# An eleventh ring slot for expert rows, paid for by halved gate matrices, shared mixer rows and four sets of V weights

## What is computed

```python
h = h + mixer(rmsnorm(h))          # RG-LRU group and mLSTM group side by side, one W_in, one W_out
h = h + peer(rmsnorm(h))           # 8 heads, 16 experts of 16384 each
y = rmsnorm(h)

# peer, for a block of 128 tokens
qh = (xb @ wq).reshape(128, 8, 2, 128)
s1, s2 = qh[:, :, 0] @ keys1.T, qh[:, :, 1] @ keys2.T     # top 16 of each, then top 16 of the 256 sums
act = gelu(einsum('td,thkd->thk', xb, u_tab[e])) * softmax(sc)
out = einsum('thk,thkd->td', act, v_tab[e])

# in the mixer's RG-LRU group: gates of 8 blocks of 64 channels
r = sigmoid(einsum('btni,nij->btnj', xb, wa) + ba);  i = sigmoid(einsum('btni,nij->btnj', xb, wx) + bx)
```

## Time and profile before

| | us |
|---|---|
| median of 3 runs | 3149.01 |
| lowest and highest run | 3145.65, 3157.63 |
| the profiled execution | 3160.47 |
| its span from first to last instruction | 3158.7 |
| PE busy | 2558.1 (81%) |
| DVE busy | 2189.3 (69%) |
| POOL busy | 2020.1 (64%) |
| ACT busy | 689.3 (22%) |

### The profile page before, as it was taken

The page is one execution under the profiler, slowest core; times in us unless marked ns, Lnnn a source line. Parts: engine busy times, 40 slices in busy tenths (PEclk is TensorE's granted clock), DMA queues, the critical chain, the costliest instruction groups (busy, mean ns, idle before and its releaser), DMA issues.

```text
span 3158.7 us, 39239 instructions
## 1 busy us (share of the span) xinstructions
PE 2558.1 (81%) x11988; PEld 1176.9 (37%) x11988; DVE 2189.3 (69%) x5635; ACT 689.3 (22%) x2526; POOL 2020.1 (64%) x2131
## 2 busy tenths in 40 slices
PE   7787889777888789777888888777987788877666
PEld 2554444233523354233523353234523353333111
DVE  2364887588756877588757887588757877688453
ACT  2121222112311122112311222112221222111112
POOL 0131667766777667766777667766776667766775
PEclk9789999988988889988988899888988899877667
DMA  7363999999999999999999999999999999999998
GB/s 268 132 204 133 384 396 400 419 419 398 391 407 419 412 382 404 419 419 395 399 418 419 418 398 400 419 418 387 401 419 419 411 394 419 418 418 380 417 420 363
DMA packets 339982, 1212.73 MB, mean 384 GB/s; under 512 B 41064, under 2 KB 41200, under 8 KB 339776
## 3 DMA queue, kind: packets, MB, share of 16 engines
q0 software_dynamic: 304128, 1107.43, 87.7%
q1 hardware_dynamic: 35648, 102.80, 8.4%
HBM read 1205.21 MB, written 4.87 MB: 383 GB/s over the span
## 4 chain that ended last, share of the span: by engine, by line
PE 37%; DMA 28%; DVE 14%; issue 10%; POOL 7%; ACT 3%; POOLq 0%; SPq 0%; DVEq 0%; ACTq 0%
PE bank L487 22%; DMA ring<-peer_v,idxv 21%; PE acc L487 14%; DMA ring<-peer_u,idx 7%; POOL ring L463 7%; DVE ring L1510 5%; ACT xn L904 1%; DVE xc L1368 1%; ACT coefv L904 1%; DVE topi L1287 1%; DVE kw L1285 1%; DVE tops L1286 0%; DVE tops L1284 0%; DVE topi L1288 0%; ACT wv L904 0%
## 5 line engine op out<-in xcount | busy, mean ns | idle before, releaser
L487 PE MATMUL acc<-ring,wv 128*32 128x512 f32 x4224 | 1276.2, 708 | 488.4 <-DMA ring<-peer_v,idxv 370.0
L1510 DVE SCALAR_TENSOR_TENSOR ring<-ring,xcur 128x1024 f32<-128x1024 f32 x1056 | 1282.7, 1219 | 543.8 <-DMA ring<-peer_u,idx 527.6
L463 POOL DMA_INDIRECT ring<-peer_u,idx x1056 | 1015.6, 962 | 626.0 <-issue 403.1
L463 POOL DMA_INDIRECT ring<-peer_v,idxv x1024 | 970.4, 948 | 444.0 <-issue 264.3
L487 PEld LDWEIGHTS acc<-ring,wv 128*32 128x32 f32 x4224 | 170.1, 115 | 1135.9 <-DMA ring<-peer_v,idxv 840.6
L487 PEld LDWEIGHTS bank<-xT,win 128*128 128x128 f32 (+1 forms) x2304 | 277.1, 191 | 100.4 <-issue 95.5
L487 PE MATMUL bank<-xT,win 128*128 128x128 f32 (+1 forms) x2304 | 308.0, 291 | 3.9 <-ACT xT L904 2.4
L904 ACT ACTIVATE wv<-rep,coefv 128x32 f32<-128x32 f32 x1024 | 258.8, 312 | 53.2 <-PE acc L487 51.6
L487 PEld LDWEIGHTS bank<-xT,qk 128*128 128x128 f32 x1024 | 159.5, 246 | 86.3 <-issue 86.3
L487 PE MATMUL bank<-win,xT 128*128 128x512 f32 (+3 forms) x368 | 187.8, 645 | 1.9 <-ACT xT L904 1.9
L487 PE MATMUL bank<-xT,qk 128*128 128x128 f32 x1024 | 172.3, 337 | 0.1
(11 more groups left out here) (231 smaller groups left out, 2251.2 us busy)
## 6 DMA issues: line engine op xcount, KB each, us to landing
qk<-wq SPq DMA_DIRECT2D x64, 512.0 KB, 6.5
t<-wq SPq DMA_DIRECT2D x64, 512.0 KB, 6.8
ring<-peer_u,idx POOLq DMA_INDIRECT x1056, 7.6
ring<-peer_v,idxv POOLq DMA_INDIRECT x1024, 7.7
win<-w_in SPq DMA_DIRECT2D x6, 2048.0 KB, 15.1
ring<-wq SPq DMA_DIRECT2D x16, 512.0 KB, 5.0
wout<-w_out SPq DMA_DIRECT2D x1, 4096.0 KB, 21.5
xn<-x_prompt SPq DMA_DIRECT2D x8, 512.0 KB
```

The costliest lines, as they stand in the source:

```text
L463: pool.indirect_dma_start(out=ring[:, slot, :], out_offset=None, in_=(peer_u, peer_v)[which], in_offset=bass.IndirectOffsetOnAxis(ap=rows_ ...
L487: return nc.tensor.matmul(out, lhsT, rhs, start=start, stop=stop)
L1510: stt(row, row, 1.0, xcur[:, :], ALU.mult, ALU.mult, accum_out=dots[:, column(b, e):column(b, e) + 1]).then_inc(s_dot, 1)
```

## The change

The ring gets an eleventh slot. The 4 KB per partition for it come from four places. `wa` and `wx` are held without their zeros, as 64 columns for each half of the partitions, so that each 128-channel product becomes two products of 64 rows and 64 columns, which write the upper and the lower half of the same bank. The two rows of `rows_hi` move into `xl`, the convolution's input, behind its first three columns. `wv` has four sets instead of eight. `ones4` is one column that is read with a step of zero. The two memsets of `wa` and `wx` and SP's wait for them go.

```diff
-RING = 10
-SETS = 8
+RING = 11
+SETS = 4
...
-        wa = sb("wa", [P, FT, P])
-        wx = sb("wx", [P, FT, P])
+        wa = sb("wa", [P, FT, P // 2])
+        wx = sb("wx", [P, FT, P // 2])
...
-        ones4 = sb("ones4", [HEADS, P])
+        ones4 = sb("ones4", [HEADS, 1])
...
-        rows_hi = sb("rows_hi", [HEADS, 2, P])
...
-        rows = [kflat[0:HEADS, P * r:P * r + P] for r in range(4)] + [rows_hi[:, 0, :], rows_hi[:, 1, :]]
+        rows = [kflat[0:HEADS, P * r:P * r + P] for r in range(4)] + [xl[0:HEADS, f, CONV_W - 1:CONV_W - 1 + P] for f in range(2)]
...
-            sp.wait_ge(s_zero, 2)
             for half in range(2):
                 lo = half * 64
-                sp.dma_start(wa[lo:lo + 64, :, lo:lo + 64], lru_wa[half]).then_inc(s_blocks, 16)
-                sp.dma_start(wx[lo:lo + 64, :, lo:lo + 64], lru_wx[half]).then_inc(s_blocks, 16)
+                sp.dma_start(wa[lo:lo + 64, :, :], lru_wa[half]).then_inc(s_blocks, 16)
+                sp.dma_start(wx[lo:lo + 64, :, :], lru_wx[half]).then_inc(s_blocks, 16)
...
-            pool.memset(wa[:, :, :], 0.0).then_inc(s_zero, 1)
-            pool.memset(wx[:, :, :], 0.0).then_inc(s_zero, 1)
...
-                    for f in range(FT):
-                        mm(by4(bA)[:, f, 0:n], wa[:, f, :], xc[:, f, 0:n])
-                    for f in range(FT):
-                        last = mm(by4(bB)[:, f, 0:n], wx[:, f, :], xc[:, f, 0:n])
+                    for to, w_gate in ((bA, wa), (bB, wx)):
+                        for f in range(FT):
+                            for lo in (0, 64):
+                                own = slice(lo, lo + 64)
+                                last = mm(by4(to)[own, f, 0:n], w_gate[own, f, :], xc[own, f, 0:n])
                     last.then_inc(s_ri_ps, 1)
...
-                    mm(bD[:, 16:20], ones4[:, :], dg4[:, :]).then_inc(s_cols_ps, 1)
+                    mm(bD[:, 16:20], spread(ones4[:, :], 1, P), dg4[:, :]).then_inc(s_cols_ps, 1)
```

More of the change, by code:

```diff
@@ L198, in program @@
         s_state_out = sem("s_state_out")
-        s_zero = sem("s_zero")
         s_blocks = sem("s_blocks")
@@ L1382, in mixer @@
                     link(stt(rows[1][:, 0:n], rows[0][:, 0:n], 0.0, rows[1][:, 0:n], ALU.max, ALU.add))
-                    link(dve.tensor_tensor_scan(rows[2][:, 0:n], ones4[:, 0:n], rows[1][:, 0:n], 0.0, ALU.mult, ALU.subtract))
+                    link(dve.tensor_tensor_scan(rows[2][:, 0:n], spread(ones4[:, :], 1, n), rows[1][:, 0:n], 0.0, ALU.mult, ALU.subtract))
                     link(stt(rows[3][:, 0:n], bB[0:HEADS, 0:n], bg[:, 0:1], rows[2][:, 0:n], ALU.add, ALU.subtract))
```

## The result

The changed kernel takes 3193.49 us (median of 4 runs, 3191.95 to 3194.92) against 3150.0 us of the kernel before (4 runs). The ratio, taken over the runs, is 1.0125, 95% interval [1.0105, 1.0144], so it is slower by 1.05 to 1.44%; the medians lie 43 us apart. 3134 us was forecast, and the range, 3116 to 3151, doesn't hold the result.

What follows compares the result with a forecast made beforehand. Transfers at 419 GB/s were taken as the bound, POOL's gather issue second. Terms -9.9 - 5.0 - 2.5 + 2.2 = -15.2 us, taken from the median 3149.01, gave 3134 us; range 3116 to 3151.

Steps and rivals of the forecast that it cites:

- I take 419 as what the transfers can do here: Loop transfers: ceiling 419 GB/s against a rate of 408, so 65 us is all that better gather supply could win.
- Small rows in the convolution's buffer, one-column ones, no memsets: Moved rows, one-column ones and two dropped memsets: same instructions, no wait added, 0 us.
- the only slower one: Rival: gate halves don't overlap their weight loads, 14.9 us a step instead of 2.2; 3157 to 3246 us, chance 0.08.
- Eleven slots: Ring: POOL stands one gather further on when held, 1.24 us once a run; -17.4 us, bounds 0 and -23.
- A: Low-rate stretch at ticks 37 to 50, in each of 8 blocks, losing 3.9 to 7.9 us; gain 9.9 us.
- C: Low-rate stretch at tick 82, in 4 blocks, losing 1.6 to 2.1 us; gain 5.0 us, bounds 0 and 8.1.
- D: Low-rate stretch at ticks 20 to 26, in 4 blocks, losing 0.9 to 1.5 us; gain 2.5 us.
- rival 1: No gain from the slot: POOL's gain before tick 50 is waited away afterwards; 3146 to 3151 us, chance 0.25.
- Gate halves: Gate step on PE, 8 matmuls become 16: +1.1 us a step, +2.2 us for two startup steps.
- sets: ACT's V-weight copies wait for the set four experts back, not eight; covered by ACT's own wait, 0 us.
- POOL's wait for PE falls: Sign that the forecast is right: POOL's loop wait for PE, 179.7 us before, gets smaller.
- about 410: Sign that the forecast is right: the loop's mean rate rises from 408 to about 410 GB/s.

Runs made afterwards that it cites:

- e1: Changed kernel with the 32-byte constant eps allocated last, so the eleven-slot ring starts on a 256-byte boundary: 3145.7 us, 0.9973 of the kernel before.
- e5: e1 with the ring back at ten slots, leaving gate halves, four sets and small rows: 3152.93 us, 0.9998 of the kernel before.
- e6: Kernel before with 256 bytes of small constants moved behind the ring, which then starts at 575 x 256: 3154.96 us, 0.9989 of before.
- e8: Kernel before with a 32-byte pad behind the ring, so only what follows the ring starts off the boundary: 3153.42 us, 0.9991 of before.
- e9: e1 with five sets of V weights instead of four, gl_a and gl_b moved to the end of memory: 3141.48 us, 0.9964 of the kernel before.
- e10: e1 with the 128-byte rep allocated first, so win and wout start on a boundary too: 3145.26 us, 0.9972 of the kernel before.
- e3: Kernel before with a 128-byte pad ahead of its ten-slot ring: 3203.46 us, 1.0159 of the kernel before.

## Why the prediction was wrong

**The step that failed** is its first: "I take 419 as what the transfers can do here". It is read rightly for the kernel before. It was then carried into the changed kernel as a constant, with bytes and rate untouched, and the whole sum was about the 65 us that lie below it. But 419 is the rate for rows that start on a 256-byte boundary; off it the rate is 409. The 60 us that the lower ceiling costs in the loop, 34 to 41 net, are in no term of the sum. They came in by the edits that were costed at 0 or only for their instructions: "Small rows in the convolution's buffer, one-column ones, no memsets" and the gate halves. 2048 of the 2528 bytes are a multiple of 256, so that the one-column ones alone, 480 bytes less, made the offset. For an edit that changes a buffer's size, the instructions are not all: every buffer behind it moves. No rival held this either; the only slower one was on the weight loads.

**Eleven slots**, -17.4 us (bounds 0 and -23): right in sign, the size about half, 8 us with an uncertainty of 7, and, as will be seen, not in the places that it was added up from. In e1, where the ceiling is as before, A, C and D can be read one by one. Stretches of e1, columns as in the earlier trace rows:

```profile
725.00:734.00 9.00, 6.00 (x38) 2.32 (x36) 7.18 (x27) 1.55 (x6) 6.86 (x8) 1.00 1.02 366
...
1238.00:1251.00 13.00, 11.60 (x66) 5.31 (x64) 9.08 (x21) 3.90 (x13) 9.03 (x10) 1.00 0.95 342
1594.00:1607.00 13.00, 10.73 (x64) 5.30 (x64) 9.23 (x22) 3.90 (x13) 9.17 (x10) 0.99 0.91 323
1841.00:1874.00 33.00, 28.25 (x198) 20.09 (x196) 28.43 (x76) 6.93 (x28) 23.09 (x25) 0.90 0.99 372
...
2185.00:2229.00 44.00, 37.79 (x241) 25.05 (x241) 37.22 (x106) 9.73 (x39) 29.21 (x31) 0.86 0.96 354
```

- A, 1.24 us in each of 8 blocks: block 4 loses 33 x (1 - 372/419) = 3.7 us, before 3.9; block 5 44 x (1 - 354/419) = 6.8, before 7.9. The sign is right and the gain is 0.2 and 1.1 in these two blocks.
- C, -5.0: not there. Block 2 loses 13 x (1 - 342/419) = 2.4 us, before 1.6 to 2.1 where there was a dip; block 3, which had none (417), loses 13 x (1 - 323/419) = 3.0.
- D, -2.5: block 1 loses 9 x (1 - 366/419) = 1.1 us, before 1.5; a gain of 0.4 where 0.6 a block was taken.

One execution is a weak witness, since blocks differ by 1 to 2 us. But seven traces have the ring on the boundary. From POOL's start of one U gather to that of another, mean of blocks 0 to 6, in us (tick 146 is tick 18 of the next block):

```
ticks             ten slots: before, e5, e6, e8    eleven: e1, e9, e10
D,  20 to 26       18.6   19.0   19.1   18.7        19.3   18.6   18.8
A,  37 to 50       39.8   38.4   40.0   40.2        38.5   38.2   38.8
    50 to 56       15.1   15.2   15.0   15.2        15.7   15.7   15.7
C,  78 to 86       21.1   20.6   20.6   21.2        21.5   21.1   20.8
    86 to 127     106.8  106.5  106.7  106.5       104.7  104.6  105.0
all, 18 to 146    352.4  351.6  352.2  352.9       351.6  350.6  350.9
```

C and D gain nothing. A gains 1.1 us on the mean up to tick 50, about the 1.24 that was taken (though e5, without the slot, stands there too), and 0.6 of it is given back right behind, as the prediction's own lower bound said ("the lead is given back at ticks 50 to 54"): "because the stalls that cost lie before tick 50" was the wrong choice, and that much of rival 1 was right. The largest gain, 1.9 us, lies in ticks 86 to 127, for which the sum has no term; what makes it stays open. Some of it is lost again, and the whole block gains 1.2 us, 10 us in 8 blocks, which agrees with the 8 above. So the right sign is in part luck.

Why C fails is to be seen in POOL and PE in order of time, block 3 of e1:

```profile
1591.28 0.94 POOL L458 DMA_INDIRECT ring<-peer_u,idx  x1 [0.30 <-issue]
1595.07 0.94 POOL L458 DMA_INDIRECT ring<-peer_v,idxv  x1 [2.85 <-issue]
```

```profile
1587.23 3.14 PE L482 MATMUL bank<-win,xT 128*128 128x512 f32 x4
1590.30 1.05 PE L482 MATMUL acc<-ring,wv 128*32 128x512 f32 x4
1591.28 1.98 PE L482 MATMUL bank<-win,xT 128*128 128x512 f32 x4
1593.19 1.05 PE L482 MATMUL acc<-ring,wv 128*32 128x512 f32 x4
```

PE ends the sum at 1593.19 + 1.05 = 1594.24, and POOL goes on 0.83 us later, as it did in the earlier trace rows; the row itself names no releaser, so that this is read from the times. POOL did get one place further, but the slot there is freed by the next sum, and between two sums PE does a projection of 1.98 us. One place is worth 1.24 us only if what holds POOL comes at POOL's pace; here it comes every 2.9 us. Instead of two waits, 2.03 us over the usual 0.30, there is one, 2.85 - 0.30 = 2.55.

Whether a block has this dip goes with TensorE's clock. The projection ahead of these sums takes 3.14 us here, where the next one takes 1.98; it took 3.37 in block 2 of the kernel before. The clock in these two stretches, first before, then e1 (PEclk, third from last):

```profile
1240.20:1243.50 3.30, 3.30 (x8) 0.96 (x6) 2.68 (x5) 1.75 (x7) 2.59 (x3) 0.57 1.04 425
1587.20:1590.40 3.20, 3.20 (x8) 1.29 (x8) 3.20 (x5) 1.30 (x6) 2.28 (x4) 0.63 1.03 422
```

So for most of it PE ran at the lower of its two levels, 1.2 GHz. In the kernel before the projection took 3.3 to 3.4 us in blocks 0, 1, 2 and 4, and POOL waited 1.8 to 2.3 us, over the usual 0.30 a gather, at ticks 80 to 84; in blocks 3, 5 and 6 it took 1.98 and POOL waited 0.15 at most. These are four blocks with the dip and three without, as the prediction counted them. In e1 the slow ones are blocks 2, 3 and 4, with waits of 2.4 to 2.6 us, against 0.9 in the others. C was counted as a fixed place of the program; it comes and goes with the clock of the execution, and the slot doesn't change that.

**Gate halves**, +2.2 (bounds 0 and +4.4 for the startup): they cost nothing; a step takes 1.97 us against 2.06, so that the lower bound of 2.2 us a step, taken from overlapping tiles, was the right one. By the rule of the Trainium skill, TensorEngine Tiling (Array Packing), Gotcha 1: PSUM Pressure, which was set against the halves, it would be 4.4 us. The trace doesn't bear it out here: two row tiles that write different partitions of one bank take no longer than the full tile did. With e5 at 0.9998, **sets** and **small rows** stay at 0 as forecast, apart from the addresses.

**Signs.** "POOL's wait for PE falls" holds: in e1 it is 139.6 us over 340 to 2830, where it was 179.7 and is 186.7 in e5 with ten slots.

```profile
POOL ring L458 <- PE acc L482: 139.6, 206, 3.0
```

A rate of "about 410" in the loop, without the offset, is 409 in e1, but also in e5 without the slot, so that it tells nothing. That "tick 82 loses its dip" fails, and "1 to 1.5 us less each" for A holds only up to tick 50. The gate step stays under 4.4 us, and ACT waits more before the V weights without harm. POOL does get one gather ahead, as was costed; but the lead is not kept, and what decided the result lay outside the sum.

Two readings of the prediction are off, without weight for its sum: the dips in the row of GB/s go down to 380, not 378; and in the table of slots it is 9 and 10 places, not 10 and 10, from V of tick 52 to tick 54.

Not settled: why a row off the boundary takes 159 to 170 ns and not a fixed time more, and why the size of the offset doesn't matter. One more piece for each row off the boundary, whatever the distance (theory 1a in the expectation of e3), would fit the equal losses; the runs show where the loss arises, not what happens inside the transfer.

## What to carry to other kernels

Where transfers are the bound, the place of their target is part of the kernel: after any change of a buffer's size, work out where each target of the main transfers now starts, and keep it on a multiple of 256 bytes. In a profile, a rate whose flat pieces change their level points to the transfers themselves, and not to a wait; look at the level before you look for a stall. And a slot more in a ring is worth one interval of the issuer only where the consumer that holds it comes at that pace, and only as long as the ring's table keeps the lead.

## What was new of the hardware

Gathered rows of 4096 bytes that start 32, 128 or 224 bytes past a multiple of 256 in SBUF move at 409 GB/s instead of 419, and the kernel takes 1.5 to 1.7% longer; at 256 bytes past a multiple of 512 there is no loss. A packet takes 159 to some 170 ns instead of a steady 159. The query weights' packets, 32 bytes off while the ring is on the boundary (e8), take a steady 159 all the same. Two 64-row tiles of TensorE that write separate partitions of one PSUM bank overlap: 32 records in 1.97 us, no more than the 2.06 us of 16 full-width ones.
